# The scale of a layer's second norm: its conditioning sums moved from TensorE in attention to VectorE under the output projection

## What is computed

```python
s_lat = silu(c)
sh1, sc1, g1, sh2, sc2, g2 = split(s_lat @ ada_w[i] + ada_b[i], 6)   # ada_w[i]: 1024 x 6144
h = modulate(x, norm_mix_g[i], sh1, sc1)        # rmsnorm(x, g) * (1 + scale) + shift
mix = concat([attention(h, ctx), pooling(h)]) @ mix_out_w    # layer 0; layer 1: Fourier mixing
x = x + g1 * mix
h = modulate(x, norm_ffn_g[i], sh2, sc2)        # <- sc2 of layer 0 is what the change is about
x = x + g2 * swiglu(h, w1, w3, w2)              # layer 0, 1024 x 2816; layer 1: top 2 of 8 experts
```

## Time and profile before

| | us |
|---|---|
| median of 3 runs | 1337.63 (1336.05 to 1337.82) |
| the profiled execution | 1337.4 |
| its span | 1335.6 |
| TensorE busy | 1303.5 (98%) |
| VectorE busy | 442.9 (33%) |
| ScalarE busy | 235.8 (18%) |
| attention, first scores to last transposition | 90.5 to 131.2 |
| output projection | 130.9 to 158.1 |
| first matmul of the dense layer | 162.9 |

### The profile page before, as it was taken

One profiled execution on the slowest core, in us unless ns is written; L12 is line 12 of the kernel. 1 busy time (PEld: TensorE's weight loads), 2 busy tenths in 40 slices (PEclk: granted clock), 3 DMA queues, 4 the chain that ended last, 5 costly groups with the idle time before them and its releaser, 6 DMA issues.

```text
span 1335.6 us, 28363 instructions
## 1 busy us (share of the span) xinstructions
PE 1303.5 (98%) x12604; PEld 680.2 (51%) x12604; DVE 442.9 (33%) x885; ACT 235.8 (18%) x397; POOL 19.1 (1%) x34
## 2 busy tenths in 40 slices
PE   6998999999999999999999999999999999999997
PEld 5865899999997333333333333433333333332333
DVE  2757589999756101120020020112003002011203
ACT  2556533433453000000000000010000000000002
POOL 0310000000000000000000000000000000000000
PEclk9999999999999999999999999999999999999999
DMA  9683289998635879998998999999799899989980
GB/s 395 255 339 143 95 326 344 383 369 329 266 143 206 330 300 386 421 420 346 422 421 353 414 420 370 399 391 420 297 422 421 357 415 421 414 354 421 421 334 34
DMA packets 59207, 457.82 MB, mean 343 GB/s; under 512 B 6736, under 2 KB 6864, under 8 KB 7760
## 3 DMA queue, kind: packets, MB, share of 16 engines
q1 hardware_dynamic: 59088, 456.02, 84.3%
HBM read 454.95 MB, written 1.05 MB: 341 GB/s over the span
## 4 chain that ended last, share of the span: by engine, by line
PE 80%; DVE 12%; DMA 3%; issue 2%; ACT 2%; SPq 0%; DVEq 0%; ACTq 0%; PEldq 0%
PE bank L1845 43%; PE bank L1858 22%; DVE work L994 5%; PE bank L1514 3%; DVE split L979 3%; DMA ring<-in_ada 2%; PE bank L1825 1%; PE bank L1476 1%; DMA ring<-in_mixa 1%; PE bank L1561 1%; PE bank L1815 1%; PE bank L1436 1%; PE bank L1764 1%; PE bank L1714 1%; PE bank L1749 1%
## 5 line engine op out<-in xcount | busy, mean ns | idle before, releaser
L1845 PE MATMUL bank<-ring,work 128*32 128x512 f32 (+1 forms) x6144 | 584.9, 539 | 1.1 <-DVE moe L1373 1.1
L1845 PEld LDWEIGHTS bank<-ring,work 128*32 128x32 f32 x6144 | 198.9, 110 | 377.2 <-issue 344.4
L1858 PE MATMUL bank<-ring,moe 128*32 128x512 f32 x2688 | 294.1, 592 | 0.0
L1373 DVE TENSOR_TENSOR moe<-moe,bank 128x256 f32<-128x256 f32 (+1 forms) x96 | 31.4, 383 | 647.8 <-ACT moe L882 647.8
L1858 PEld LDWEIGHTS bank<-ring,moe 128*32 128x32 f32 x2688 | 87.2, 110 | 197.8 <-issue 196.4
L882 ACT ACTIVATE moe<-bank 128x256 f32<-128x256 f32 (+1 forms) x96 | 27.4, 357 | 795.4 <-PE bank L1845 795.4
L1714 PE MATMUL bank<-split 128*128 128x256 f32 x1056 | 131.0, 284 | 0.2
L1714 PEld LDWEIGHTS bank<-split 128*128 128x128 f32 x1056 | 128.0, 192 | 2.3 <-ACT split L799 1.3
L979 DVE TENSOR_TENSOR split<-ring,split 128x2048 fp32r<-128x2048 f32 x33 | 75.5, 2289 | 11.1 <-PE bank L1514 6.0
L805 ACT ACTIVATE split<-ring 128x2048 fp32r<-128x2048 f32 x32 | 61.3, 1915 | 86.5 <-PE bank L1714 75.9
L994 DVE SCALAR_TENSOR_TENSOR work<-ring,condp,work 128x512 f32<-128x512 f32 x98 | 73.7, 752 | 5.1 <-DMA ring<-in_ada 1.3
(11 more groups left out here) (233 smaller groups left out, 677.2 us busy)
## 6 DMA issues: line engine op xcount, KB each, us to landing
ring<-in_moe SPq DMA_DIRECT2D x336, 1024.0 KB, 12.6
ring<-in_ffn SPq DMA_DIRECT2D x16, 2048.0 KB, 8.8
ring<-in_ada SPq DMA_DIRECT2D x28, 1024.0 KB, 7.2
ring<-in_ada SPq DMA_DIRECT2D x10, 2048.0 KB, 12.1
ring<-in_mixout SPq DMA_DIRECT2D x2, 2048.0 KB, 8.2
ring<-in_fnet SPq DMA_DIRECT2D x2, 2048.0 KB, 9.3
ring<-in_mixa SPq DMA_DIRECT2D x1, 2048.0 KB, 13.0
ring<-in_mixb SPq DMA_DIRECT2D x1, 1664.0 KB, 11.8
```

The lines of the kernel that those rows point to most:

```text
L1373: nc.vector.tensor_tensor(gate_e[:, g, 0:n], gate_e[:, g, 0:n], bank[g][:, n:2 * n], ALU.mult).then_inc(e_hidden, 1)
L1845: last = mm(bank[g][c * QUAD:(c + 1) * QUAD, 0:count * P], x_group[:, 4 * half + k, j * CAP + g * QUAD:j * CAP + (g + 1) * QUAD], source[: ...
L1858: last = mm(bank[3 + n][c * QUAD:(c + 1) * QUAD, :], hiddenT[phase % 2][:, g, blk * QUAD:(blk + 1) * QUAD], source[:, j, n * 512:(n + 1) * ...
```

## The change

The two units of sc2 are no longer multiplied by TensorE. `scale_unit` lets VectorE form their weighted sums into a place of its own, one ahead of the low part of the fifth piece of the output projection and one ahead of the sixth; `sum_scaled` sums both over the partitions on TensorE after the seventh piece; `take_scaled` turns them and adds the bias on VectorE, after the last low part. The code in attention goes (both units, the turn, `take_rows` and `take_ada` for it). In the ring the two units now come behind the two of the output projection.

```diff
-        for part in (1, 2):
-            add_ada(part)
+        add_ada(1)
         for n in range(2):
             add("mixout", mixout_d[n], KD * 512)
+        add_ada(2)
         for n in range(DENSE_UNITS):
...
-        ADA_ITEMS = {1: (2, 0), 3: (2, 1)}
-        ADA_TAKES = {2: 1.5, 4: 2, 6: 2.5}
+        ADA_TAKES = {2: 1.5}
...
+            def scale_unit(n):
+                u = first_unit[f"ada2_{n}"]
+                unit_wait(dve, u)
+                w = view(ring, unit_slot(u) * UNIT, KD, 512)
+                total = scaled_sum[:, n, :]
+                link(nc.vector.tensor_scalar(total, w[:, 0, :], cond[:, 0, 0:1], None, ALU.mult))
+                for k in range(1, KD):
+                    ins = nc.vector.scalar_tensor_tensor(out=total, in0=w[:, k, :], scalar=cond[:, k, 0:1], in1=total,
+                                                         op0=ALU.mult, op1=ALU.add)
+                    if k < KD - 1:
+                        link(ins)
+                ins.then_inc(scaled_summed, 1)
+                dve.wait_ge(scaled_summed, n + 1)
+                dve.sem_inc(unit_free[unit_slot(u)], 1)
+            def take_scaled():
+                dve.wait_ge(ada_ready, NRUNS)
+                n, at = 8, 64
+                link(nc.vector.transpose(sum_turned[:, 0:QUAD * n], bank[2][:, 0:QUAD * n]))
+                link(nc.vector.tensor_reduce(small[:, 0:n], sum_turned[:, 0:QUAD * n].rearrange("p (a b) -> p a b", b=QUAD), AX_X, ALU.add))
...
             attended(HEADS // 2 - 1)
+            scale_unit(0)
+            mixer_lows("mixout", len(EARLY_MIX), len(EARLY_MIX) + 1)
+            scale_unit(1)
+            mixer_lows("mixout", len(EARLY_MIX) + 1)
+            take_scaled()
             modulation(2, "ffn_g", 0, 0, 4)
-            mixer_lows("mixout", len(EARLY_MIX))
             add_projected("mixout", MIX_BANKS, 0, 2)
...
+            def sum_scaled():
+                pe.wait_ge(scaled_summed, 2)
+                for n in range(2):
+                    rows = scaled_sum[:, n, :].rearrange("p (j q c) -> p j q c", j=4, q=4)
+                    for q in range(4):
+                        last = mm(bank[2][q * QUAD:(q + 1) * QUAD, n * P:(n + 1) * P], C("quad"), rows[:, :, q, :],
+                                  start=True, stop=True)
+                last.then_inc(ada_ready, 1)
...
                     last.then_inc(mixer_used, 1)
+                    if name == "mixout" and m == first_piece[name] + 6:
+                        sum_scaled()
...
-                if n in ADA_ITEMS:
-                    ada_unit(*ADA_ITEMS[n])
-                if n == 5:
-                    ada_turn(2)
```

More of the change, by code:

```diff
@@ L271, in build @@
         router = view(work, 3456, KD, EXPERTS)
+        scaled_sum = view(moe, 0, 2, 512)
         ada_sum, sum_turned = view(work, 0, SUM_BUFFERS, 512), view(work, 512 * SUM_BUFFERS, 512)
@@ L360, in build @@
         half_in, half_free = [sem(f"half_in{n}") for n in range(2)], [sem(f"half_free{n}") for n in range(2)]
-        sum_ready = sem("sum_ready")
+        sum_ready, scaled_summed = sem("sum_ready"), sem("scaled_summed")
         dve_step, pool_step = sem("dve_step"), sem("pool_step")
@@ L473, in build @@
         CHAN_BANKS, ROW_BANKS = (1, 3, 0, 4, 5, 6, 7, 2), (1, 3, 0, 2)
-        RUNS = [(part, (0, 1) if part == 2 else (0, 1, 2, 3), 6, 7) for part in range(PARTS)]
+        RUNS = [(0, (0, 1, 2, 3), 6, 7), (1, (0, 1, 2, 3), 6, 7)]
+        NRUNS = len(RUNS) + 1
         SUM_BANKS = (2, 3, 2, 3)
@@ L1001, in add_half @@
                     dve.sem_inc(sum_ready, 1)
+            def scale_unit(n):
[17 more added lines that the diff above has]
+                link(nc.vector.tensor_reduce(small[:, 0:n], sum_turned[:, 0:QUAD * n].rearrange("p (a b) -> p a b", b=QUAD), AX_X, ALU.add))
+                link(nc.vector.tensor_tensor(ada[:, at:at + 2 * n].rearrange("p (a b) -> p a b", b=2)[:, :, 0], small[:, 0:n],
+                                             V("ada_b")[:, at // 2:at // 2 + n], ALU.add))
+                dve.sem_inc(ada_taken, 1)
             def take_sums(r):
@@ L1660, in _ @@
                     pe.wait_ge(pool_in, 16)
-                    pe.wait_ge(ada_taken, PARTS)
+                    pe.wait_ge(ada_taken, NRUNS - 1)
                     for g in range(NG):
```

## The result

| | before | changed |
|---|---|---|
| median, us | 1336.84 (1335.83 to 1337.82, 4 runs) | 1345.27 (1344.43 to 1349.47, 4 runs) |
| the profiled execution, us | 1337.4 | 1345.46 |
| its span, us | 1335.6 | 1343.6 |

The ratio is 1.0068, 95% interval 1.0056 to 1.0081: 7.5 to 10.8 us slower. Predicted were 1346.4 and +8.8 us. Counts of matmuls in the text are counts of records of the profile, as in the prediction.

The account below looks back on a forecast made before the run. Attention was taken as a loop of mutual waits, projection and dense layer as TensorE-bound; -3.5 (attention) + 9.9 (late dense unit) + 2.4 (clock) = +8.8 us, so 1346.4 us, range 1342.5 to 1351.5.

Parts of the forecast that it names:

- Attention, 3.5 us: In attention, two conditioning units leave TensorE and a copy leaves VectorE, ending waits for score matmuls: 3.5 us gained.
- Scaling, 6.0 us a unit: On VectorE in the output projection, a unit's tensor_scalar and seven multiply-adds take 6.0 us.
- wait in m5, 1.8: In output projection piece m5 (of m0 to m7), TensorE waits 1.8 us for VectorE's low half.
- The issue at some 150 us, and the landing 7.8 later: First dense unit's load waits in slot 2 for m7's low half, issues at some 150 us, lands 7.8 us later.
- The gap, nearly 8 us: Ahead of the means in the output projection's last piece, TensorE stands idle nearly 8 us, awaiting the late load.
- the 2.4 us in front: In the output projection, m5's wait and summing the scaled units cost 2.4 us, swallowed by the late load's wait.
- The clock, 2.4 us: After TensorE's idle time, low clock slows the means and m7b, the last piece's second half: 2.4 us.
- The rival with the clock up: Clock stays at full speed after the idle time ahead of the means: +6.4 us, 1344.0; chance 0.18.
- Dense at 162.9 + 8.8 = 171.7: The dense layer's first matmul, at 162.90 us before, comes later by the forecast's sum of 8.8 us.
- Whatever delays its first matmul delays the end by as much.: In the dense layer TensorE is always busy, so a delay of its first matmul passes whole to the end.
- The rival "in time": Slot 2 frees by 144.5 us, so the first dense load isn't late: -1.1 us, 1336.5; chance 0.09 with its faster form.
- Its form without the wait in m5: First dense load in time and no TensorE wait in m5: -3.5 + 0.6, 1334.7; half of the 0.09 chance.

Follow-up runs that it names:

- lows first: The changed kernel with VectorE making the low halves of m4 and m5 both ahead of the second scaling unit: 1348.26 us, ratio 1.0092 to before.
- gap filled: Matmuls of no use put in TensorE's idle time ahead of the means: changed kernel 1345.33 us; with m4 and m5 low halves before second scaling unit, 1345.66.
- ring in turn: The changed kernel with output and conditioning units alternating in the ring, ahead of the first dense unit: 1341.07 us, ratio 1.0032 to before.
- turn late: Changed kernel with alternating ring units, m4 and m5 low halves before second scaling unit, and VectorE's turn of sums after its additions to x: 1335.09 us, ratio 0.9990.

## Why the prediction held

- **Attention, 3.5 us.** Measured 3.2. Both waits went; VectorE's reduction at 96.10 comes at 95.28, and the copy is gone.
- **Scaling, 6.0 us a unit; wait in m5, 1.8.** 6.0 and 1.92. That both were covered by the load is shown by the profile of the kernel with the lows first.
- **The issue at some 150 us, and the landing 7.8 later.** 150.58 and 7.9. One load in the trace of before, with nothing ahead of it, priced this one. One reading beside it was wrong and entered no sum: the load of before was issued 47 us ahead of its use, but took 9.3 us to land, so it lay ready some 38 us and not 47.
- **The gap, nearly 8 us.** 7.69. As the text had it, nothing of the 2.4 us in front was paid beside it.
- **The clock, 2.4 us.** 2.5, by the means and m7b, in the profile; with the gap filled the profiles got 2.0 and 1.5 us back, and no median did. The fall was recorded in the gap: 0.72 over 156 to 158, and 0.50 behind it. The row of the granted clock at the start of the kernel reads full speed while the first 16 matmuls take 5.56 us instead of 3.69, and was the wrong one to trust. The Trainium skill ("TensorE: Matmul & The Clock Gate", Part 1) says that the default is throttled and that activity releases it; this trace agrees. The rival with the clock up is out in the trace; its time, 1344.0, is nearly as close to the median as mine.
- **Dense at 162.9 + 8.8 = 171.7.** It is 172.82. Attention gave 0.3 less, issue and landing took 0.3 more, means and m7b 0.5.
- **"Whatever delays its first matmul delays the end by as much."** This step was wrong by 1.9 us. The dense layer kept the delay and added 0.2; but I took all behind it as the same in both kernels, while 1.7 of the 8.89 us of Fourier matmuls in the profile of before was low clock, which the page's row of 40 slices doesn't show, and 0.4 came back among the experts, for which the rows name no reason. That the sum of 8.8 is so close to the 8.1 of the profiles is in part luck: errors of +1.1 and -1.9 stand against each other.
- **The rival "in time".** With the ring in turn the load is in time, and the time isn't the 1336.5 I gave but 1341.07: the rival left out the clock behind m5's wait and the turn ahead of the additions. Its form without the wait in m5, 1334.7, became 1337.69, and 1335.09 only with the turn late.

## What to carry to other kernels

In a ring of buffers, moving a load moves the buffer's next user too: before moving weights, write down for each slot who frees it now and when, what stands ahead of that release in its engine's queue, and add a load's time. Work put "under" an engine is only free where nothing behind it in its own queue is awaited; ask for the due time of each item behind it. And if a change opens a pause on TensorE, price the pause and the low clock behind it, and look in the baseline for pauses that are already charged so.

## What the runs showed that I had not expected

- The granted clock falls behind short pauses too: 1.92 us in m5 (in 3 of the 4 profiles with this wait), 1.7 us in attention (2 of the 10 that have no units there), and ahead of the Fourier stage, where TensorE does a few small matmuls and then stands idle for 0.87 us (6 of the 11 without a filler). Each costs 1.2 to 1.7 us unless a longer wait follows, and in the same kernel one execution has it and the next hasn't.
- The dense layer takes 191.0 to 193.4 us, and the longer it is, the longer VectorE waits for halves of the conditioning weights: 1.3 us in the profile of before, 3.1 at 193.1, 3.6 at 193.4. VectorE is busy 95% there, so it has little to cover a late load of 1 MB with; that these waits make the layer longer is read from the profiles, no run tests it. What makes these loads late in some executions stays open.
